# A row of token factors taken to all partitions: matmul with a ones matrix, or a row in DRAM

## What is computed

```python
    y_ssm = _rmsnorm(y_ssm, ssm_ng).astype(x.dtype)
    ...
    y_att = _rmsnorm(o * jax.nn.silu(z_att.astype(jnp.float32)), att_ng).astype(x.dtype)
    y = jnp.concatenate([y_ssm, y_att], axis=-1)
    x = x + (y @ w_out).astype(x.dtype)
```

## Time and profile before

| | us |
|---|---|
| median of three runs | 1929.95 |
| the three runs | 1929.95, 1927.86, 1930.5 |
| the profiled execution | 1928.19 |
| its span, first to last instruction | 1926.6 |

### The profile page before, as it was taken

The page is one execution under the profiler, slowest core; times in us unless marked ns, Lnnn a source line. Parts: engine busy times, 40 slices in busy tenths (PEclk is TensorE's granted clock), DMA queues, the critical chain, the costliest instruction groups (busy, mean ns, idle before and its releaser), DMA issues.

```text
span 1926.6 us, 32969 instructions
## 1 busy us (share of the span) xinstructions
PE 1896.8 (98%) x11368; PEld 1773.8 (92%) x11368; DVE 1137.6 (59%) x2189; ACT 709.2 (37%) x1395; POOL 441.0 (23%) x756
## 2 busy tenths in 40 slices
PE   5999999999999999999999999999999999999999
PEld 4899999999999999999999999999999997888877
DVE  7865665556455564545645456455566566776664
ACT  6422333333243334333343333343345443333341
POOL 5874445556112002020020200202002010100121
PEclk9999999999999999999999999999999999999999
DMA  9343343444325224132141321423338454432573
GB/s 226 105 119 108 109 109 101 120 127 123 93 74 168 84 60 143 54 108 79 55 149 57 105 80 55 139 68 94 93 99 276 153 200 139 133 122 98 180 257 122
DMA packets 212055, 230.50 MB, mean 120 GB/s; under 512 B 33978, under 2 KB 167188, under 8 KB 210772
## 3 DMA queue, kind: packets, MB, share of 16 engines
q1 hardware_dynamic: 185392, 143.58, 26.5%
q0 software_dynamic: 21072, 74.93, 11.7%
q10 hardware_dynamic: 5524, 11.14, 1.6%
HBM read 166.83 MB, written 62.74 MB: 119 GB/s over the span
## 4 chain that ended last, share of the span: by engine, by line
PE 94%; DVE 4%; DMA 1%; issue 0%; ACT 0%; SPq 0%; POOL 0%; POOLq 0%; DVEq 0%; ACTq 0%
PE GB L195 61%; PE TB L2350 3%; PE TB L2482 3%; PE TB L2483 3%; PE TB L2484 3%; PE TB L2371 3%; PE GB L2482 2%; PE GB L2483 2%; PE GB L2484 2%; PE TB L2392 2%; PE TB L1137 1%; PE TB L1147 1%; PE TB L1148 1%; PE TB L2411 1%; DVE XL L673 1%; PE TB L2336 0%
## 5 line engine op out<-in xcount | busy, mean ns | idle before, releaser
L195 PE MATMUL GB<-XH,whi 128*128 128x384 f32 x2448 | 827.6, 338 | 1.0 <-ACT QR L1740 0.8
L195 PE MATMUL GB<-XH,wlo 128*128 128x384 f32 x2448 | 800.5, 327 | 0.0
L195 PE MATMUL GB<-XL,whi 128*128 128x384 f32 x2448 | 798.0, 326 | 0.0
L195 PEld LDWEIGHTS GB<-XH,whi 128*128 128x128 f32 x2448 | 459.9, 188 | 14.2 <-issue 8.9
L183 DVE TENSOR_TENSOR wlo<-wraw,whi 128x256 fp32r<-128x256 f32 x412 | 201.9, 493 | 456.4 <-ACT whi L179 451.3
L195 PEld LDWEIGHTS GB<-XL,whi 128*128 128x128 f32 x2448 | 460.2, 188 | 5.3 <-issue 3.8
L195 PEld LDWEIGHTS GB<-XH,wlo 128*128 128x128 f32 x2448 | 459.3, 188 | 0.0
L179 ACT CAST whi<-wraw 128x256 fp32r<-128x256 f32 x412 | 166.5, 405 | 644.8 <-PE GB L195 634.3
L2089 DVE RECIPROCAL SQ<-SQ 128x136 f32<-128x136 f32 x128 | 127.7, 997 | 1.4
L1787 ACT ACTIVATE PR<-PR,nmx 128x128 f32<-128x128 f32 (+8 forms) x72 | 53.4, 742 | 184.4 <-DVE nmx L2060 171.8
L1545 POOL DMA_DIRECT2D t_s<-TS x16 | 11.7, 733 | 360.9 <-DVE TS L1978 311.7
(11 more groups left out here) (517 smaller groups left out, 2877.2 us busy)
## 6 DMA issues: line engine op xcount, KB each, us to landing
wraw<-in_w_in SPq DMA_DIRECT2D x380, 128.0 KB, 2.2
TS<-in_w_out POOLq DMA_DIRECT2D x32, 512.0 KB, 5.6
t_s<-TS POOLq DMA_DIRECT2D x16, 1024.0 KB, 4.8
AREA<-in_w_out SPq DMA_DIRECT2D x34, 256.0 KB, 3.2
AREA<-in_x_prompt POOLq DMA_DIRECT2D x32, 256.0 KB, 4.8
AREA<-t_s SPq DMA_DIRECT2D x30, 256.0 KB, 2.7
out_y_prompt<-AREA POOLq DMA_DIRECT2D x28, 256.0 KB, 3.1
xt<-in_x_prompt SPq DMA_DIRECT2D x5, 1024.0 KB, 5.4
```

The lines of the kernel that those rows point to most:

```text
L195: ins = T.matmul(group(GB if bank is None else bank, b), w[:, s % SPL, kk], x[:, k + kk, c:c + n], start=first and kk == 0 and i == 0, sto ...
```

## The change

`diagonal`, PE's `spread` and ACT's `spread` go away. POOL gets a `spread(w)`: it waits for the factors, writes the 1024 factors of `rm` as one row of a DRAM tensor `rn_s` (each element is a piece of 4 bytes, since neighbours in the row come from different partitions), waits for that to land, and loads the row with stride 0 into all 128 partitions of `RR[w]`. `norm` waits for that load (`r_in`). `spread(1)` stands ahead of the residual loads for group 0; `spread(0)` stands where the wait for PE's spread stood, ahead of those for group 1.

```diff
+    rn_s = scratch("rn_s", [2, SEQ])
...
-            SPREAD_AT = {3: 1, 5: 0}
...
+                def spread(w):
+
+                    pool.wait_ge(f["rs"], stands["rs"] + 2 - w)
+                    pool.dma_start(rn_s[w].rearrange("(m p) -> p m", p=P), rm[:, 2, w, 0:TT - 1],
+                                   allow_slow_non_contiguous=True).then_inc(f["r_out"], 16)
+                    pool.wait_ge(f["r_out"], 16 * (2 - w))
+                    pool.dma_start(RR[w], rn_s[w:w + 1, :].to_broadcast([P, SEQ])).then_inc(f["r_in"], 16)
...
+                spread(1)
                 pool.wait_ge(e["o_mm"], NR * NH)
                 residual("c11", 0, BX[0], x0)
                 pool.wait_ge(W.mm, W.multiplied(OUT0 - 1))
                 sample_in("sl", 0, x0)
-                pool.wait_ge(f["r_mm"], stands["r_mm"] + 1)
+                spread(0)
...
-                def spread(w):
-
-                    act.wait_ge(f["r_mm"], stands["r_mm"] + 2 - w)
-                    S.copy(RR[w], TB[:, 1024:1024 + SEQ]).then_inc(f["r_copy"], 1)
...
-                    dve.wait_ge(f["r_copy"], stands["r_copy"] + 2 - w)
+                    dve.wait_ge(f["r_in"], 16 * (2 - w))
...
-                def diagonal(w):
-
-                    dve.wait_ge(f["rs"], stands["rs"] + 3 - 2 * w)
-                    V.tensor_tensor(DD[w], ident[:].rearrange("p (o c) -> p o c", o=1).to_broadcast([P, TT - 1, P]),
-                                    rm[:, 2, w, 0:TT - 1].rearrange("p (m o) -> p m o", o=1).to_broadcast([P, TT - 1, P]),
-                                    ALU.mult).then_inc(f["rs"], 1)
...
-                def spread(w):
-
-                    pe.wait_ge(f["rs"], stands["rs"] + 4 - 2 * w)
-                    if not w:
-                        pe.wait_ge(f["r_copy"], stands["r_copy"] + 1)
-                    for b in range(2):
-                        ins = T.matmul(TB[:, 1024 + NW * b:1024 + NW * (b + 1)], onesr[:].bitcast(f32),
-                                       DD[w][:, 4 * b:4 * b + 4].rearrange("p m c -> p (m c)"), start=True, stop=True)
-                    ins.then_inc(f["r_mm"], 1)
...
-                    elif a in (5, 6):
-                        pe.wait_ge(f["r_copy"], stands["r_copy"] + 2)
```

More of the change, by code:

```diff
@@ L1227, in attention @@
             onames = ("ahi", "alo", "shi", "slo", "mix", "u_copy", "ss", "ms", "rt", "rs", "hi", "lo", "freed", "acc", "tmp",
-                      "ev", "r_mm")
+                      "ev")
             f = {n: free_sem(n) for n in onames}
-            f.update((n, sem("out_" + n)) for n in ("x_in0", "x_in1", "o_out0", "o_out1", "end_out", "mid", "fin", "r_copy"))
-            stands["r_copy"] = 0
+            f.update((n, sem("out_" + n)) for n in ("x_in0", "x_in1", "o_out0", "o_out1", "end_out", "mid", "fin", "r_out", "r_in"))
             e.update((n, sem("att_" + n)) for n in ("ts_in", "ts_d", "ts_out"))
@@ L1255, in attention @@
             RR = [area(AREA, at, [SEQ]) for at in (4096, 24576)]
-            DD = [area(AREA, at, [TT - 1, P]) for at in (12544, 29952)]
             BX = [area(AREA, 39424, [4, NW]), VV[1]]
@@ L1855, in scalar @@
                 root(0)
-                spread(1)
                 out_hi(7)
                 out_hi(8)
-                spread(0)
                 done = 9
@@ L2137, in take_sample @@
                     dve.wait_ge(f["acc"], stands["acc"] + acc_of(g, t) + 1)
-                    dve.wait_ge(f["rs"], stands["rs"] + 4)
+                    dve.wait_ge(f["rs"], stands["rs"] + 2)
                     dve.wait_ge(f[f"x_in{g % 2}"], {0: 80, 1: 80, 2: 80, 3: 80, 10: 160, 11: 96}[g])
@@ L2197, in vector @@
                 scales(1)
-                diagonal(1)
                 out_lo(5)
@@ L2201, in vector @@
                 scales(0)
-                diagonal(0)
                 out_lo(7)
@@ L2502, in tensor @@
                         sums(SUM_AT[i])
-                    if g == 0 and i in SPREAD_AT:
-                        spread(SPREAD_AT[i])
             return sync, scalar, vector, gpsimd, tensor
```

## The result

| | before | after |
|---|---|---|
| median, 20 runs each side by side | 1929.42 us | 1932.09 us |
| lowest and highest | 1926.15 to 1932.31 | 1929.65 to 1937.03 |
| ratio of the runs after to before, 95% interval | | 1.0019 [1.0012, 1.0027] |
| profiled execution, span | 1928.19, 1926.6 | 1936.5, 1934.9 |

By the medians the kernel became slower by 2.7 us (0.14%; the ratio over all runs gives 0.19%), where 3.4 us less had been forecast. The difference is small, under 0.2%, but the interval of the ratio excludes 1, and 1932.09 lies outside the range of the prediction, 1923.9 to 1929.4. The profiled execution of after is one of its slowest, 4.4 us above its median; what that means is worked out further down.

A forecast was written before the change was run, and what follows sets the result against it. The prediction took PE's own work to bound the kernel. Removing two spreads of 1.72 us, with no new wait counted, took 3.44 us from the median of 1929.95 us: 1926.5 us, range 1923.9 to 1929.4.

The forecast's parts named there:

- What bounds the kernel: Output stage: PE waits for nobody, so a microsecond of PE's own work there is a microsecond of the end.
- what goes from PE: PE between pieces in the output stage: two spreads go, 1.72 us each, 3.44 us together, all on the path.
- What comes in on POOL: POOL's write and broadcast of each row of factors: 7.6 us a factor, bounds 5.4 and 15.2 us; no cost expected.
- The sentence on `norm`: DVE's `norm`: neither waits in the expected case; at worst the first is up to 1.5 us late, not PE's time.
- The next thing that can be late: Ninth accumulator, `take(0, 0)`: piece 11's weights must land within 5.9 us of issue; no wait taken, upper bound 1.7 us.
- Rival 1: Ninth accumulator: piece 11's weights again take 7.6 us, PE waits 1.7 us, time 1928.2 us; chance 0.17.
- Rival 2: Behind the sums of squares: one low clock stretch more or fewer, 1.6 us, median 1924.9 or 1928.1; chance 0.14.
- Rival 3: POOL's 4-byte pieces served one by one, 20 ns each; row late for piece 9, time 1934 us; chance 0.06.
- The sum: Whole kernel: median 1929.95 us less 3.44 us of PE work gives 1926.5 us, 0.18% less.

The follow-up runs named there:

- y3: Kernel after, with the residual loads of group 1 held back until DVE has taken the first accumulator out: 1934.55 us, ratio 1.0026.
- y2: Kernel before plus one unread write of 1024 4-byte pieces, issued by POOL ahead of the residual loads of group 1: 1938.09 us, ratio 1.0045.
- y4: Kernel after itself, unchanged, measured once more with another profile: 1932.32 us, ratio 1.0017.
- x1: Kernel after, with the residual loads of group 0 issued ahead of the first write of factors: 1932.85 us, ratio 1.0011.
- x4: Kernel after, but PE transposes factors, POOL writes 512-byte pieces, group 0 residual goes ahead of the first write, group 1 waits for `take(0, 0)`: 1925.44 us, ratio 0.9974.

## Why the prediction was wrong, point by point

**What bounds the kernel, and what goes from PE: right.** PE's time counts one for one, both gaps are 0.23 us, and the account above finds 3.4 of the 3.44 us.

**What comes in on POOL: the step that failed.** It took the write at 2.7 us from the row of 1024 pieces of 32 bytes, with an upper bound of 7.6 us. The writes took 8.8 and 16.3 us, so even the bound was too low, and 9.2 us is what one costs with nothing beside it. Number of pieces and bytes were both in view; that the price rises as the piece shrinks, 2.7, 3.3, 4.2 and 9.2 us for 32, 16, 8 and 4 bytes, was not. The consequences by the prediction's own points: the first broadcast went out at 1599.65 and not near 1591, the second at 1619.42 and not by 1600, and residual group 1 at 1619.95 and not by 1602. The sentence on `norm` fell too: DVE did wait for the broadcast, 2.73 us at 1605.80:

```profile
1605.80 1.42 DVE L1988 SCALAR_TENSOR_TENSOR XHF<-ZR,vec,AREA 128x512 f32<-128x512 f32 x2 [2.73 <-DMA AREA<-rn_s]
```

In this trace PE did not notice: with 7.8 us of DVE work between the row and the take, as in y3, the accumulator would have been free at 1614.4, and PE asked for it only at 1615.60, since a late start and two low stretches of the clock had held it back. In y3 it asked at 1610.76 and waited 3.9 us for the row alone. Here the prediction had a second thing wrong. It wanted the row by 1610.7, for piece 9, and took 1.5 us of lateness as not yet PE's time. But the take stands behind all nine `norm` of this row: for an accumulator at 1612.3 the row must be in 8.6 us earlier, by 1603.7, 15.3 us after the factors and not 22.3.

**The next thing that can be late: right place, wrong traffic.** The prediction named the ninth accumulator, `take(0, 0)` and the weights of piece 11, and added up 2.7 MB in front of them. It left the 4 KB of the write out of this sum, since by bytes they are nothing. But once they are being written little else moves: 25 GB/s in y2 from 1609.3, with 1.7 MB waiting. (In after the second write had been issued at 1602.85, yet 390 GB/s moved from 1605 to 1610; its transfers began only at 1609.68, and the rate fell behind them.) The load took 12.1 us against 5.9 allowed, which gives a lateness of 6.2; PE waited 5.8. Rival 1 put an upper bound of 1.7 us on this wait, again because it took the slowest landing of before for the slowest possible.

**Rival 2, the clock.** Low stretches behind the sums came as before and once more (0.83 and 0.66 in the rows above), within what the rival allowed. Not foreseen was the stretch at the end of the wait: 6.8 us at the lower level, of which PE worked 5.83, and that cost 2.9 us on top of the 5.8. y2 and y4 have the same, 6.8 us at 0.50, of which PE worked 5.2 and 5.0 us, 2.6 and 2.5 us on top. Behind the shorter waits of x1 and y3 (5.1 and 3.9 us) the stretch cost 1.7. The Trainium skill ("TensorE: Matmul & The Clock Gate", Part 1) has PE fall back to the 1.2 GHz level after it has stood idle. The traces agree: the clock fell at 1620.40, in the 5.8 us wait of after. The prediction should have priced the wait of a rival with such a stretch.

**Rival 3, the write of single elements: the cause, at chance 0.06 and with the wrong way to PE.** It asked when the row is late for piece 9, and found that this needs over 20 us. The write did its damage sideways, to loads of another queue behind it, and by the row at the accumulator, where 15.3 us are enough. Its 20 ns a piece was a what-if; measured alone, 1024 pieces took 9.2 us, which is 9 ns a piece. The Trainium skill ("DMA: Bandwidth & Descriptors", Specifications) warns of pieces under 512 bytes, and I set that against the 32-byte row and let the row decide. The runs agree with the warning in direction; 32 and 4 bytes both lie under its 512, and cost 2.7 and 9.2 us. Whether read-modify-write is what makes the small ones dear, no run here shows; only the times by size are shown.

**The sum.** For the profiled executions: 3.44 less, 5.8 of wait, 1.7 for the low clock behind the second sums and 2.9 for that behind the wait more, and a stage that starts 1.6 us later (1579.99 against 1578.39), which the change does not touch. That is 8.6 against a difference of 8.3 in span. The medians are 2.7 us apart, 6.1 us from the 3.44 us less that were forecast. Most likely these 6.1 us are the same waits and stretches, smaller than in this profile; the runs without a profile can't show it.

**Still open.** x4 is 4.9 us below before (by its interval 3.3 to 6.8), more than the removed work of 3.44 less two transposes of 0.1, which is at the lower end of that interval; what the rest is, no run shows. That the second write of after takes 16.3 us and not 9.2 is mostly queueing behind the residual loads (its transfers began 6.8 to 9.0 us after the issue), and the 32-byte write at the same place also rose, from 1.7 to 6.7 us. What happens in the 7 us between a 4-byte write's last transfer record and its landing, and why other queues stand still in them, no run takes apart.

## What to carry to other kernels

Before layout work moves from PE to a DMA, look at the smallest piece that the DMA writes, and price it by a transfer with that piece size; if the trace has none, the nearest one is no upper bound. Charge the transfer also with what is issued behind it on any queue, and put it where the next loads have slack: two 4 KB writes at 1589 and 1594 us cost nothing that could be measured, one at 1604 cost 8.5 us. For the deadline of what the write delivers, add up all the work of the next engine between it and PE, not only the first piece. If elements must be regrouped, a PE transpose of 128x8 (0.1 us here) and 8 pieces of 512 bytes (2.1 to 2.7 us with no bulk load in front) are cheap.

## What the runs showed of the hardware

- A DRAM write of 1024 pieces takes 9.2 us for pieces of 4 bytes, 4.2 for 8, 3.3 for 16 and 2.7 for 32. Reading back 1024 pieces of 4 bytes takes 2.9 us. SP's queue is no better than POOL's (9.7 us).
- Such a write holds up transfers of other queues: a 256 KB load took 10.8 us in place of 3.2. The write's transfer records end 7 us before it lands (0.05 of DMA share while it runs alone), so the share does not show the price; issue to landing does.
- Waits of PE of 5.6 to 6.9 us (y2, after, y4) each end in 6.8 us at the 1.2 GHz level, which cost 2.5 to 2.9 us on top of the wait; waits of 3.9 and 5.1 us (y3, x1) were followed by 3.4 us of it, 1.7 us.
